# A two-block transformer kernel whose weight ring goes from four to six half slots, with the low parts written over the loaded weights

## The chip, the core and the metric

The kernel runs on one core of a Trainium2 chip. The metric is the device time of one execution in microseconds (us). The engines named below are PE (matrix multiplies; PEld is its weight load), DVE (vector), ACT (scalar, activation functions), POOL (general purpose) and SP (here it only issues the loads of the weights). Each has its own stream of instructions, run strictly in the order of the program; they wait for each other by semaphores.

## The reference

Two kinds of transformer layer, two layers of each, on 256 tokens of width 1024, everything in float32. Cut to what matters here:

```python
# first block, per layer (DEPTH = 2)
h = rms_norm(x, pre_mix_g);   x = x + rms_norm(parallel_mixer(h, ...) , post_mix_g)      # w_in, w_out
h = rms_norm(x, pre_cross_g); x = x + rms_norm(memory_cross_attention(h, mem_n, ...), post_cross_g)  # w_cq, w_ck, w_cv, w_co
h = rms_norm(x, pre_ffn_g);   x = x + rms_norm(swiglu(h, w_gate, w_up, w_down), post_ffn_g)
# second block, per layer (DEPTH = 2)
h = rms_norm_2(x, ffn1_norm); x = x + 0.5 * swiglu_2(h, ffn1_w_gate, ffn1_w_up, ffn1_w_down)
h = rms_norm_2(x, mix_norm);  (queries, keys, values, gates) = split(h @ w_in)
x = x + (g0 * (y_nsa @ w_up_nsa) + g1 * (y_sb @ w_up_sb) + g2 * (y_swa @ w_up_swa)) @ w_out
h = rms_norm_2(x, ffn2_norm); x = x + 0.5 * swiglu_2(h, ffn2_w_gate, ffn2_w_up, ffn2_w_down)
```

Nearly all of the arithmetic is products of the 256 tokens with weight matrices of width or depth 1024 or 2816.

## The kernel before, in words

All large weights are laid out by the host as one stream of 332 **slots** of 1024 x 256 numbers (1 MB), in the order in which they are needed (`ORDER`; names such as `fq0`, `wo3` are columns of a projection, `gate`, `up`, `down` with a number are parts of an FFN). Each slot is two **halves** of 512 KB, so there are 664 halves.

A float32 product is made of three faster ones: a number is split into a high part (rounded by a copy to the type fp32r) and a low part (what is left). A half therefore goes through four stations:

1. SP loads it into `raw[m % RING]` (L1874). The ring has RING = 4 such buffers.
2. ACT copies it to `w_hi` (`split_hi`, L779).
3. DVE writes `raw - w_hi` to `w_lo` (`split_lo`, L1234).
4. PE multiplies (L259): 24 matmuls a half, and the last one counts up the semaphore `half_used`.

`w_hi` and `w_lo` are rings of four, too. In before, SP loads half m into its `raw` buffer as soon as DVE has made the low part of half m - 4 (`lo_done`), whether PE has used that half or not. ACT, ahead of splitting half m, waits for the load and for `half_used` of half m - 4, since `w_hi` is overwritten.

When a slot is split is set by hand: the program of ACT and of DVE calls `ahead(name)` where slot `name` is being used, and that splits the slot after it. In a run of projections the order on DVE is `ahead(X)`, read the result of X, `ahead(Y)`, read the result of Y. In an FFN, `ahead` stands between the activations, and the eleven `ahead(("down", j))` stand together, after the last activation. Behind the last of them follows at once what ends the layer's part: in the first block `norm_add` (ACT squares the four pairs of output tiles, DVE and PE sum them, ACT takes the root, DVE scales and adds to `x`), in the second block `half_update` (DVE scales and adds straight away), and then `norm_in` (ACT makes the high parts `xn_hi` of the next input, DVE the low parts `xn_lo`), for which PE waits. Output projections (`wo`, `co`) are four slots in a row, with their four `ahead` calls together and then `norm_add` or an addition. PE's last `down` slot is ordered so that its output pairs end one after the other (`down_made`), so that these steps can begin while PE still multiplies.

Of the kernel before, what the change touches and what calls it, by code (L numbers as in the profile page):

```python
# [7 lines left out]
F32 = mybir.dt.float32  # L8
F32R = mybir.dt.float32r
# [5 lines left out]
P = 128  # L15
# [12 lines left out]
COLS = 256  # L28
SLOT = KT * COLS
HK = KT // 2  # L30
RING = 4
N_CMP = (S - 32) // 16 + 1
N_CMP0 = (P - 32) // 16 + 1
VEC = 3 * P
# [13 lines left out]
ORDER = []  # L48
# [4 lines left out]
SLOT_AT = {name: n for n, name in enumerate(ORDER)}  # L53
N_SLOTS = len(ORDER)
# [38 lines left out]
def build(nc, A):  # L93
    T, AC, V, G, SY = nc.tensor, nc.scalar, nc.vector, nc.gpsimd, nc.sync
# [3 lines left out]
    def sb(name, shape, dt=F32):  # L98
        return nc.alloc_sbuf_tensor(name, shape, dt)[tuple(slice(None) for _ in shape)]

    def sb_at(name, shape, dt, offset):
        return nc.alloc_sbuf_tensor_at(name, shape, dt, offset=offset)[tuple(slice(None) for _ in shape)]

    base = (nc.sbuf_base + 31) // 32 * 32
    shared = 13 * 2048 + 24 * 1024 + 16384
    nc.alloc_sbuf_tensor("shared", [P, shared // 4 + 16], F32)

    proj = sb_at("proj", [P, 13, 2, COLS], F32, base)
    gates = sb_at("gates", [P, 24, S], F32, base + 13 * 2048)
# [6 lines left out]
    mem_lo = sb_at("mem_lo", [P, KT, S], F32R, base + 13 * 2048 + 24 * 1024 + 8192)  # L116
    table = sb_at("table", [P, 12, S], F32, base + 13 * 2048 + 24 * 1024)

    raw = [sb(f"raw{r}", [P, HK, COLS]) for r in range(RING)]
    w_hi = [sb(f"w_hi{r}", [P, HK, COLS], F32R) for r in range(RING)]  # L120
    w_lo = [sb(f"w_lo{r}", [P, HK, COLS], F32R) for r in range(RING)]
    x = sb("x", [P, KT, S])
    xn = sb("xn", [P, KT, S])
    xn_hi, xn_lo = sb("xn_hi", [P, KT, S], F32R), sb("xn_lo", [P, KT, S], F32R)
# [70 lines left out]
    hi_done, lo_done, half_used = sig("hi_done"), sig("lo_done"), sig("half_used")  # L195
# [575 lines left out]
    def scalar_program():  # L771
        own = sig("act_own")

        def split_hi(name):
            for m in (2 * SLOT_AT[name], 2 * SLOT_AT[name] + 1):
                AC.wait_ge(*loaded[m % RING].at(m // RING + 1))
                if m >= RING:
                    AC.wait_ge(*half_used.at(m - RING + 1))
                AC.activation(w_hi[m % RING], raw[m % RING], ACT.Copy).then_inc(*hi_done.next())  # L779

        def ahead(name):

            if SLOT_AT[name] + 1 < N_SLOTS:
                split_hi(ORDER[SLOT_AT[name] + 1])

        def load_sqrt():
            AC.activation(scale_col[:, 2:3], eps, ACT.Sqrt)
# [75 lines left out]
            AC.activation(out, probT[1][:, 1, S:2 * S], ACT.Sin).then_inc(*trig_made.next())  # L863
        AC.wait_ge(*vec_made.at(1))
        AC.activation(vec_sb, bank[1][0:12, 0:VEC], ACT.Copy, scale=8.0).then_inc(*vec_copied.next())
        split_hi(ORDER[0])

        for L in range(DEPTH):
            at = lambda name: ("b1", L, name)
# [142 lines left out]
        for L in range(DEPTH, 2 * DEPTH):  # L1012
# [51 lines left out]
            m = mix_out.at(7 * l + 4)  # L1064
# [157 lines left out]
    def vector_program():  # L1222
# [8 lines left out]
        def split_lo(name):  # L1231
            for m in (2 * SLOT_AT[name], 2 * SLOT_AT[name] + 1):
                V.wait_ge(*hi_done.at(m + 1))
                V.tensor_tensor(w_lo[m % RING], raw[m % RING], w_hi[m % RING].bitcast(F32), ALU.subtract  # L1234
                                ).then_inc(*lo_done.next())

        def ahead(name):
            if SLOT_AT[name] + 1 < N_SLOTS:
                split_lo(ORDER[SLOT_AT[name] + 1])

        def low_half(lo, src, hi, ready, to):

# [110 lines left out]
        for b in range(4):  # L1353
            for k in (2 * b, 2 * b + 1):
                m = V.scalar_tensor_tensor(xn[:, k, :], xn[:, k, :], c("mem_g")[:, k:k + 1], rinv[:, 0, :],
                                           ALU.mult, ALU.mult)
# [1 line left out]
            V.wait_ge(*mem_normed.last())  # L1358
            low_half(mem_lo[:, pair_of(b), :], xn[:, pair_of(b), :], mem_hi[:, pair_of(b), :], mem_hi_done.at(b + 1),
                     mem_split)  # L1360
        split_lo(ORDER[0])

        update = None
        for L in range(DEPTH):
# [49 lines left out]
            for ct in range(2):  # L1414
                w = lambda n: small[:, SM1["conv_w"].start + 2 * n + ct:SM1["conv_w"].start + 2 * n + ct + 1]
                m = V.tensor_scalar(xc[:, ct, :], lx[:, ct, :], w(3), small_1("conv_b")[:, ct:ct + 1], ALU.mult, ALU.add)
# [453 lines left out]
    def sync_program():  # L1870
        for m in range(2 * N_SLOTS):
            if m >= RING:
                SY.wait_ge(*lo_done.at(m - RING + 1))
            SY.dma_start(raw[m % RING], A["stream"][m].rearrange("p (k c) -> p k c", k=HK)  # L1874
                         ).then_inc(*loaded[m % RING].next())

# [174 lines left out]
```

## Time and profile before

| | |
|---|---|
| median of 3 runs | 2480.09 us (2479.8 to 2481.58) |
| the profiled execution | 2480.8 us; span of the profile 2478.9 us |
| mean granted TensorE clock | 0.948 |
| PE busy | 2221.4 us (90%) |
| DVE busy | 1430.3 us (58%) |
| ACT busy | 1137.6 us (46%) |
| POOL busy | 83.8 us (3%) |
| loads of the stream | 664 of 512 KB, 144 GB/s read over the span |

Busy time is the time in which the engine had an instruction running. Only PE is near the whole span; the other engines are on the path where PE waits for them. Times in rows of a timeline are us from the span's start.

### The profile page before, as it was taken

What the parts mean: (1) busy time and instruction counts of PE and PEld (TensorE: products, weight loads), DVE (VectorE), ACT (ScalarE), POOL (GpSimd) and SP (SyncE); (2) the same over time, 40 slices, a digit from 0 to 9 for tenths busy, and PEclk for the clock granted to TensorE, in tenths of its full rate; (3) what the DMA queues carried; (4) which work ended last, traced back from release to release, by engine and by line L of the source; (5) the groups of instructions that cost most, each with busy time, mean ns of one, the idle gap of its engine ahead of it and who ended that gap; (6) DMA issues with size and microseconds to landing.
All of it is one profiled execution on the core that took longest, in us unless ns stands there. A gap on an engine that the chain in (4) does not pass through costs nothing.

```text
span 2478.9 us, 40437 instructions
## 1 busy us (share of the span) xinstructions
PE 2221.4 (90%) x17158; PEld 2126.7 (86%) x17158; DVE 1430.3 (58%) x2194; ACT 1137.6 (46%) x1745; POOL 83.8 (3%) x81
## 2 busy tenths in 40 slices
PE   3888879998988799979998998899999988988999
PEld 2877779998868799979997877899899988878999
DVE  3454656546546565465557556655556575556654
ACT  3354444443545444444445456444444444465442
POOL 4000000000000000010000000000000000000000
PEclk9888899998989999989999899999999998989999
DMA  5632425554423255645644223456456543234554
GB/s 131 188 102 84 137 83 179 186 187 136 131 74 130 96 164 181 204 145 184 200 141 153 86 79 109 158 184 194 150 187 193 165 153 102 86 103 133 176 186 153
DMA packets 97956, 360.28 MB, mean 145 GB/s; under 512 B 11064, under 2 KB 11065, under 8 KB 97264
## 3 DMA queue, kind: packets, MB, share of 16 engines
q1 hardware_dynamic: 95616, 348.17, 43.4%
q0 software_dynamic: 1728, 6.38, 1.3%
q8 instruction: 135, 2.21, 0.4%
q10 hardware_dynamic: 432, 3.15, 0.3%
q14 instruction: 45, 0.37, 0.0%
HBM read 354.25 MB, written 3.41 MB: 144 GB/s over the span
## 4 chain that ended last, share of the span: by engine, by line
PE 74%; DVE 13%; ACT 7%; issue 2%; POOL 2%; DMA 2%; ACTq 0%; DVEq 0%; POOLq 0%
PE bank L259 65%; DVE w_lo L1234 3%; ACT w_hi L779 2%; PE bank L311 1%; POOL sq L1803 1%; DMA raw<-in_stream 1%; PE bank L295 1%; PE bank L639 1%; DVE sq L1287 1%; DVE xn_lo L1260 1%; PE bank L316 1%; DVE x L1291 1%; DVE sq L1771 1%; PE bank L312 1%; ACT sq L790 0%
## 5 line engine op out<-in xcount | busy, mean ns | idle before, releaser
L259 PE MATMUL bank<-xn_hi,w_hi 128*128 128x256 f32 x3296 | 959.1, 291 | 136.6 <-DVE xn_lo L1260 103.9
L1234 DVE TENSOR_TENSOR w_lo<-raw,w_hi 128x1024 fp32r<-128x1024 f32 x664 | 809.9, 1252 | 470.1 <-ACT w_hi L779 469.9
L259 PE MATMUL bank<-xn_lo,w_hi 128*128 128x256 f32 x3296 | 950.2, 288 | 0.0
L259 PE MATMUL bank<-xn_hi,w_lo 128*128 128x256 f32 x3296 | 949.1, 288 | 0.0
L779 ACT ACTIVATE w_hi<-raw 128x1024 fp32r<-128x1024 f32 x664 | 674.2, 1050 | 339.2 <-PE bank L259 321.0
L259 PEld LDWEIGHTS bank<-xn_hi,w_hi 128*128 128x128 f32 x3296 | 651.4, 198 | 151.7 <-issue 137.7
L259 PEld LDWEIGHTS bank<-xn_lo,w_hi 128*128 128x128 f32 x3296 | 651.4, 198 | 0.2
L259 PEld LDWEIGHTS bank<-xn_hi,w_lo 128*128 128x128 f32 x3296 | 650.6, 197 | 0.0
L259 PE MATMUL bank<-hid_hi,w_hi 128*128 128x256 f32 x1056 | 291.5, 276 | 0.0
L259 PE MATMUL bank<-hid_lo,w_hi 128*128 128x256 f32 x1056 | 291.5, 276 | 0.0
L259 PE MATMUL bank<-hid_hi,w_lo 128*128 128x256 f32 x1056 | 291.5, 276 | 0.0
L259 PEld LDWEIGHTS bank<-hid_lo,w_hi 128*128 128x128 f32 x1056 | 198.3, 188 | 0.0
L259 PEld LDWEIGHTS bank<-hid_hi,w_hi 128*128 128x128 f32 x1056 | 198.3, 188 | 0.0
L259 PEld LDWEIGHTS bank<-hid_hi,w_lo 128*128 128x128 f32 x1056 | 198.2, 188 | 0.0
L831 ACT ACTIVATE hid_hi<-act_t 128x512 fp32r<-128x512 f32 x66 | 41.7, 632 | 206.0 <-DVE act_t L1305 206.0
L827 ACT ACTIVATE act_t<-act_t 128x512 f32<-128x512 f32 x66 | 41.7, 632 | 197.8 <-DVE act_t L1300 197.8
L259 PE MATMUL bank<-y_hi,w_hi 128*128 128x256 f32 x384 | 110.3, 287 | 12.2 <-DVE y_lo L1244 4.5
L259 PE MATMUL bank<-y_lo,w_hi 128*128 128x256 f32 x384 | 109.2, 284 | 0.0
L1803 POOL TENSOR_TENSOR sq<-sq 128x512 f32<-128x512 f32 x36 | 55.9, 1553 | 1574.7 <-ACT sq L790 1571.2
L259 PE MATMUL bank<-y_hi,w_lo 128*128 128x256 f32 x384 | 109.1, 284 | 0.0
L259 PEld LDWEIGHTS bank<-y_hi,w_hi 128*128 128x128 f32 x384 | 74.2, 193 | 14.6 <-issue 7.1
L1305 DVE TENSOR_TENSOR act_t<-act_t,bank 128x512 f32<-128x512 f32 x66 | 45.3, 686 | 63.7 <-PE bank L259 63.7
(338 smaller groups left out, 2562.8 us busy)
## 6 DMA issues: line engine op xcount, KB each, us to landing
raw<-in_stream SPq DMA_DIRECT2D x664, 512.0 KB, 4.2
skew<-logit POOLq DMA_DIRECT2D x1, 2304.0 KB, 35.2
table<-skew POOLq DMA_DIRECT2D x1, 1408.0 KB, 7.4
logit<-in_small POOLq DMA_DIRECT2D x4, 288.5 KB, 3.1
con<-in_con ACTq DMA_DIRECT2D x1, 1029.0 KB, 7.1
xn<-in_mem ACTq DMA_DIRECT2D x1, 1024.0 KB, 11.6
x<-in_x ACTq DMA_DIRECT2D x1, 1024.0 KB, 14.9
out<-x POOLq DMA_DIRECT2D x1, 1024.0 KB, 4.2
```

Source lines behind the costliest of these rows:

```text
L259: m = T.matmul(out, a, b, start=first and j == 0, stop=True, skip_group_check=True)
L295: m = T.matmul(out, avg, sq[:, k, :], start=k == 0, stop=k == 1)
L311: T.matmul(out, v_of(0), pT[:, 0:S], start=first, stop=False, skip_group_check=True)
L312: return T.matmul(out[:, P:S], v_of(1), pT[:, S:S + P], start=False, stop=last, skip_group_check=True)
L316: m = T.transpose(dst[:, to * P:(to + 1) * P], src[:, frm:frm + P], c("ident"))
L639: T.matmul(out[:, LATE], q[:, P:S], k, start=True, stop=True)
L779: AC.activation(w_hi[m % RING], raw[m % RING], ACT.Copy).then_inc(*hi_done.next())
L827: AC.activation(act_t, act_t, ACT.Silu).then_inc(*silu_made.next())
L831: AC.activation(hid_hi[:, 2 * j:2 * j + 2, :], act_t, ACT.Copy).then_inc(*hid_hi_made.next())
L1234: V.tensor_tensor(w_lo[m % RING], raw[m % RING], w_hi[m % RING].bitcast(F32), ALU.subtract).then_inc(*lo_done.next())
L1305: V.tensor_tensor(act_t, act_t, dense[1], ALU.mult).then_inc(*up_read.next())
L1803: G.tensor_tensor(sq[:, 0:2, :], sq[:, 0:2, :], sq[:, pair_of(b), :], ALU.add).then_inc(*summed.next())
```

## The change

RING becomes 6. `w_lo[r]` gets the same addresses as `raw[r]`: DVE subtracts in place, so the low part overwrites the loaded half, and one buffer stands for two. Since the buffer now holds what PE reads, SP may load half m only when PE has used half m - 6 (`half_used`), where it waited for `lo_done` of half m - 4. ACT's own wait for `half_used` is dropped: the load that it waits for implies it. `ahead(name)` now splits the slot two after `name`, and both ORDER[0] and ORDER[1] are split ahead of the first layer.

```diff
-RING = 4
+RING = 6
...
-    nc.alloc_sbuf_tensor("shared", [P, shared // 4 + 16], F32)
+    nc.alloc_sbuf_tensor("shared", [P, shared // 4 + 16 + RING * SLOT // 2], F32)
...
-    raw = [sb(f"raw{r}", [P, HK, COLS]) for r in range(RING)]
+    raw_at = base + shared + 64
+    raw = [sb_at(f"raw{r}", [P, HK, COLS], F32, raw_at + r * SLOT * 2) for r in range(RING)]
     w_hi = [sb(f"w_hi{r}", [P, HK, COLS], F32R) for r in range(RING)]
-    w_lo = [sb(f"w_lo{r}", [P, HK, COLS], F32R) for r in range(RING)]
+
+    w_lo = [sb_at(f"w_lo{r}", [P, HK, COLS], F32R, raw_at + r * SLOT * 2) for r in range(RING)]
...
                 AC.wait_ge(*loaded[m % RING].at(m // RING + 1))
-                if m >= RING:
-                    AC.wait_ge(*half_used.at(m - RING + 1))
                 AC.activation(w_hi[m % RING], raw[m % RING], ACT.Copy).then_inc(*hi_done.next())
...
-            if SLOT_AT[name] + 1 < N_SLOTS:
-                split_hi(ORDER[SLOT_AT[name] + 1])
+            if SLOT_AT[name] + 2 < N_SLOTS:
+                split_hi(ORDER[SLOT_AT[name] + 2])
...
-        split_hi(ORDER[0])
+        for n in range(2):
+            split_hi(ORDER[n])
...
             if m >= RING:
-                SY.wait_ge(*lo_done.at(m - RING + 1))
+                SY.wait_ge(*half_used.at(m - RING + 1))
```

(The same two edits are made for `split_lo` on DVE.) What moves on the engines is seen at three places. In these rows `raw2_66` and `w_lo2_72` are `raw[2]` and `w_lo[2]`; lines are those of the kernel in question.

SP, the loads behind the first ones, before:

```order
L1874 DMA raw3<-in_stream 128x1024
L1874 DMA raw0<-in_stream 128x1024 [waits lo_done]
L1874 DMA raw1<-in_stream 128x1024 [waits lo_done]
L1874 DMA raw2<-in_stream 128x1024 [waits lo_done]
L1874 DMA raw3<-in_stream 128x1024 [waits lo_done]
```

and now:

```order
L1876 DMA raw3_67<-in_stream 128x1024
L1876 DMA raw4_68<-in_stream 128x1024
L1876 DMA raw5_69<-in_stream 128x1024
L1876 DMA raw0_64<-in_stream 128x1024 [waits half_used]
L1876 DMA raw1_65<-in_stream 128x1024 [waits half_used]
```

Two more loads go out without a wait, and all later ones wait for PE in place of DVE.

ACT, the end of the second block's first FFN (the last two `ahead` calls of the `down` slots, then `norm_in`), before:

```order
L779 ACTIVATE w_hi0<-raw0 128x1024 [waits half_used,loaded0]
L779 ACTIVATE w_hi1<-raw1 128x1024 [waits half_used,loaded1]
L779 ACTIVATE w_hi2<-raw2 128x1024 [waits half_used,loaded2]
L779 ACTIVATE w_hi3<-raw3 128x1024 [waits half_used,loaded3]
L787 ACT_TABLE_LOAD
L787 ACTIVATE scale_col<-eps_t 128x1
L799 ACTIVATE xn_hi<-x,small 128x256 [waits x_updated]
```

and now:

```order
L779 ACTIVATE w_hi0<-raw0_64 128x1024 [waits loaded0]
L779 ACTIVATE w_hi1<-raw1_65 128x1024 [waits loaded1]
L779 ACTIVATE w_hi2<-raw2_66 128x1024 [waits loaded2]
L779 ACTIVATE w_hi3<-raw3_67 128x1024 [waits loaded3]
L787 ACT_TABLE_LOAD
L787 ACTIVATE scale_col<-eps_t 128x1
L799 ACTIVATE xn_hi<-x,small 128x256 [waits x_updated]
```

The number of splits in front of `norm_in` is the same; they are of the slots one further on, and each waits for a load alone. That load itself waits for PE.

DVE, the first projections (`proj` from bank0 and bank1 are the results of `fq0` and `fq1`), before:

```order
L1234 TENSOR_TENSOR w_lo2<-raw2,w_hi2 128x1024 [waits hi_done]
L1234 TENSOR_TENSOR w_lo3<-raw3,w_hi3 128x1024 [waits hi_done]
L1266 RECIPROCAL scale<-root 128x256 [waits rooted]
L1268 RECIPROCAL scale_col<-scale_col 128x2
L1234 TENSOR_TENSOR w_lo0<-raw0,w_hi0 128x1024 [waits hi_done,dve_own]
L1234 TENSOR_TENSOR w_lo1<-raw1,w_hi1 128x1024 [waits hi_done]
L1378 TENSOR_TENSOR proj_49<-bank0,scale 128x512 [waits half_used]
L1378 TENSOR_TENSOR proj_49<-bank1,scale 128x512 [waits half_used]
```

and now:

```order
L1235 TENSOR_TENSOR w_lo4_74<-raw4_68,w_hi4 128x1024 [waits hi_done]
L1235 TENSOR_TENSOR w_lo5_75<-raw5_69,w_hi5 128x1024 [waits hi_done]
L1267 RECIPROCAL scale<-root 128x256 [waits rooted]
L1269 RECIPROCAL scale_col<-scale_col 128x2
L1235 TENSOR_TENSOR w_lo0_70<-raw0_64,w_hi0 128x1024 [waits hi_done,dve_own]
L1235 TENSOR_TENSOR w_lo1_71<-raw1_65,w_hi1 128x1024 [waits hi_done]
L1380 TENSOR_TENSOR proj_49<-bank0,scale 128x512 [waits half_used]
L1380 TENSOR_TENSOR proj_49<-bank1,scale 128x512 [waits half_used]
```

The pair of splits in front of the first `proj` was halves 4 and 5 and is now halves 6 and 7, whose loads can only start when PE has used halves 0 and 1.

## Rows read from the trace of the kernel before

**Rows 1.** Waits, whole program: us in total, times, longest

```profile
ACT w_hi L779 <- PE bank L259: 321.0, 193, 3.7
...
PE bank L259 <- DVE xn_lo L1260: 103.9, 12, 26.2
...
PE bank L259 <- DVE w_lo L1234: 32.5, 28, 3.2
...
ACT w_hi L779 <- DMA raw<-in_stream: 18.1, 5, 6.8
```

**Rows 2.** Stretches of gate/up and down slots: us, busy per engine, PEclk, DMA, GB/s

```profile
370.00:490.00 120.00, 119.70 (x995) 119.43 (x994) 72.06 (x74) 54.87 (x65) 0.00 (x0) 1.00 0.57 184
490.00:552.00 62.00, 62.00 (x548) 61.96 (x546) 30.99 (x29) 26.72 (x28) 0.00 (x0) 1.00 0.64 204
```

**Rows 3.** Tile raw, loads' landing in stretches 500:545, 331:350, 42:58

```profile
DMA to landing us min/median/max: 4.2/4.3/4.8
...
DMA to landing us min/median/max: 3.2/3.3/3.7
...
DMA to landing us min/median/max: 22.0/23.1/27.8
```

**Rows 4.** Timelines of ACT, DVE, PE at 1256 to 1266: start, us, what, [idle before]

```profile
1256.91 1.06 ACT L779 ACTIVATE w_hi<-raw 128x1024 fp32r<-128x1024 f32 x1 [1.66 <-PE bank L259]
...
1258.01 1.23 DVE L1234 TENSOR_TENSOR w_lo<-raw,w_hi 128x1024 fp32r<-128x1024 f32 x1 [1.49 <-ACT w_hi L779]
1259.15 0.68 DVE L1329 SCALAR_TENSOR_TENSOR sq<-bank,scale 128x512 f32<-128x512 f32 x1
...
1264.94 0.36 PE L259 MATMUL bank<-xn_hi,w_hi 128*128 128x256 f32 x1 [2.69 <-DVE xn_lo L1260]
```

**Rows 5.** Timeline of ACT, 546 to 553

```profile
546.81 1.06 ACT L779 ACTIVATE w_hi<-raw 128x1024 fp32r<-128x1024 f32 x1 [1.66 <-PE bank L259]
547.89 1.28 ACT L787 ACT_TABLE_LOAD   x1
...
552.19 0.60 ACT L790 ACTIVATE sq<-bank 128x512 f32<-128x512 f32 x1 [0.76 <-PE bank L259]
```

**Rows 6.** Timeline of ACT, 262 to 268

```profile
262.12 1.06 ACT L779 ACTIVATE w_hi<-raw 128x1024 fp32r<-128x1024 f32 x1 [1.82 <-PE bank L259]
...
264.61 1.56 ACT L790 ACTIVATE sq<-bank 128x512 f32<-128x512 f32 x3
267.82 0.60 ACT L790 ACTIVATE sq<-bank 128x512 f32<-128x512 f32 x1 [1.66 <-PE bank L259]
```

**Rows 7.** Timelines of ACT and DVE, 120 to 127

```profile
120.13 1.06 ACT L779 ACTIVATE w_hi<-raw 128x1024 fp32r<-128x1024 f32 x1 [0.38 <-PE bank L259]
...
122.37 0.41 DVE L1391 TENSOR_TENSOR act_t<-bank,scale 8x256 f32<-8x256 f32 x1
...
126.56 0.49 ACT L886 ACTIVATE act_t<-act_t,small 8x256 f32<-8x256 f32 x1
```

**Rows 8.** Timeline of PE and POOL, the first 75 us; DMA issues

```profile
46.77 0.55 PE L259 MATMUL bank<-xn_hi,w_hi 128*128 128x256 f32 x1 [26.17 <-DVE xn_lo L1260]
...
74.28 0.58 PE L259 MATMUL bank<-xn_hi,w_hi 128*128 128x256 f32 x1 [11.64 <-DVE proj L1378]
...
40.38 1.21 POOL L1844 DMA_DIRECT2D skew<-logit  x1 [1.12 <-ACT logit L865]
...
skew<-logit POOLq DMA_DIRECT2D x1, 2304.0 KB, 35.2
```

**Rows 9.** Waits of PE, 1296:1356, and busy time of 1310:1325

```profile
PE bank L259 <- DVE w_lo L1234: 6.1, 5, 3.2
PE bank L612 <- ACT root L1029: 2.6, 1, 2.6
...
1310.00:1325.00 15.00, 11.44 (x78) 10.43 (x79) 13.73 (x21) 4.96 (x6) 0.00 (x0) 0.89 0.47 147
```

**Rows 10.** Timeline of PE, 1967 to 1976

```profile
1970.59 0.55 PE L259 MATMUL bank<-xn_hi,w_hi 128*128 128x256 f32 x1 [2.69 <-DVE xn_lo L1260]
```

More of the change, by code:

```diff
@@ L1237, in ahead @@
         def ahead(name):
-            if SLOT_AT[name] + 1 < N_SLOTS:
-                split_lo(ORDER[SLOT_AT[name] + 1])
+            if SLOT_AT[name] + 2 < N_SLOTS:
+                split_lo(ORDER[SLOT_AT[name] + 2])
         def low_half(lo, src, hi, ready, to):
@@ L1360, in vector_program @@
                      mem_split)
-        split_lo(ORDER[0])
+        for n in range(2):
+            split_lo(ORDER[n])
         update = None
```

## The prediction

> **What bounds the kernel now.** I read the list of waits first. PE is busy for 90% of the span, so the question is what it waits for. Its longest wait is for `xn_lo`, the input of the next group of projections: 103.9 us in 12 places. Waits for a low part of a weight, which an earlier split could remove, are 32.5 us in 28 places [rows 1]. The same list says how the weights are fed: ACT waits 193 times, 321.0 us together, for PE to free a half, but only 5 times, 18.1 us, for a load. In before, loads are so far ahead that nobody sees them.
>
> Next the stretches. In gate/up slots PE runs 995 matmuls in 120 us with no gap, in down slots 548 in 62 us [rows 2]. With 24 matmuls a half, that is 2.89 and 2.72 us a half, 5.8 and 5.4 us a slot, and the granted clock is 1.00. There is nothing to win inside these runs. Time is lost at their ends, where the timelines show ACT or DVE still splitting weights and turning to the next step as soon as they are done: the last split ends on DVE at 1259.2, and the update of x begins in the same moment [rows 4].
>
> **The step that decides.** In after, `ahead(name)` splits slot n+2, whose second half takes the buffer of slot n-1's second half. In before, the same call splits slot n+1 into the buffer of that same half. So ACT and DVE reach the same point of their programs, and wait for PE to finish the same half. But before, the data lay ready; now its load is issued only then. Each split that was released by PE is released one transfer later. The transfer takes 4.3 us in a stretch of down slots and 3.3 us in one of output slots [rows 3].
>
> **Inside a dense run this is hidden.** From `half_used` to the low part: 3.3 or 4.3 for the load, 1.06 on ACT, 1.23 on DVE, some 0.1 between them, so 5.7 to 6.7 us, while PE needs the half five halves later, 13.6 to 14.4 us. Reads of results that stand behind the split come at most 1 us late, and PE has a slot of slack for them. The cover would be gone with a transfer of over 11 us.
>
> **At the end of a run it isn't.** What follows the last `ahead` there is late by the transfer, less what ACT or DVE waited for anyway:
>
> - Second block, end of an FFN with another stage behind it, three times (the last FFN has no slot left to split). ACT's last copy starts at 1256.91, the moment PE frees the half. In after it starts 4.35 later, and so does DVE's 1259.15 update; DVE is at work without a break from there to the `xn_lo` that lets PE start at 1264.94 [rows 4]. +4.35 each, **+13.1**.
> - First block, end of the FFN, twice. ACT's copy at 546.81 is followed by a table load of 1.28 and four squares, the last of which begins at 552.19, when PE is done [rows 5]. In after: 546.8 + 4.35 + 1.06 + 1.28 + 0.1 = 553.6, and three squares at 0.52 (three take 1.56 [rows 6]) put the last at 555.2. +3.0 each, **+6.0**.
> - First block, `wo` and `co`, four times. Same reckoning from 262.12 with transfers of 3.3 to 3.8: the last square at 262.1 + 3.3 + 1.06 + 1.28 + 0.1 + 1.56 = 269.4 to 269.9, for 267.82 [rows 6]. +1.9 each, **+7.6**.
> - Second block, `wo`, twice. ACT waits there for the whole slot in any case. Copy and table load end 3.3 + 1.06 + 1.28 = 5.6 after the half, the slot after 5.8. What is left is one addition of x on DVE, about 0.6. **+1.2**, bounds 0 and 2.6 (the latter if the load takes 4.3 and a second addition is late).
> - The forget gate `f`, twice. Its read on DVE, at 122.37, stands behind a split released by PE at 120.1; with a load of about 4.6 (three loads are asked for 1.4 us apart) it comes at 127.1, and PE's `fv1` and ACT's 126.56 step wait for it [rows 7]. ACT had slack of 4 us; 0.6 to 1.2 remains. **+1.8**.
>
> **The start.** Two more halves are split on DVE ahead of the first norm, 2 x 1.23, so the first matmul moves from 46.77 to 49.2. That is only delay ahead of a stall: PE waits until 74.28 for `proj`, which waits for halves 4 and 5, loaded in 22 to 28 us while the `skew` write runs, 35.2 us from 40.4 [rows 3, 8]. In after those two come early, but the split ahead of that `proj` is of halves 6 and 7, asked for when PE has used halves 0 and 1, near 55 and 58, and the write runs to 75.6. Best case, a load with nothing before it lands by 70; worst, at 81. I take 74.1, which with 1.06, 1.23 and two reads gives 76.7. **+2.4**, bounds -1 and +6.
>
> **What the earlier split gains.** Of the 32.5 us of [rows 1], 6.1 lie in the second block's run from `sk` to `sv`, and as much in the second layer. But DVE is busy 13.7 of 15 us there and PE's next wait, for ACT's root, already takes 2.6 [rows 9]: most of what PE wins it waits for one step later. The exception is the copy of `nv`, for which ACT waits; it comes earlier. Followed through, the root comes 2.5 to 3 us sooner. I take 2.5 a layer, **-5.0**, bounds -7 and -1. The other waits for low parts stand in front of a wait for the same DVE (`merged`, the first softmax) and give nothing.
>
> **Clock.** Longer gaps mean more restarts at the lower level. The same gap of 2.69 is followed once by a matmul of 0.36 and once by one of 0.55 [rows 4, 10]. A half at 1.2 GHz takes some 5 us for 2.9. At two or three places a gap of 3 grows to 5 to 7. **+2**, bounds 0 and 6.
>
> In-place writing I cost at nothing: the subtraction reads and writes as many bytes as before, in 1.23 us, and PE's slots cover it; if it took 0.1 us more or less, only the 13 places above would show it, 1 us in all. The dropped ACT wait is replaced by the longer one.
>
> **Sum.** 13.1 + 6.0 + 7.6 + 1.2 + 1.8 + 2.4 - 5.0 + 2.0 = 29.1 on the profiled execution's 2480.8, which is 0.7 above the median. 2509.9, or **2509 us** against the median, 1.2% slower.
>
> **A rule.** The Trainium skill (DMA: Bandwidth & Descriptors, Rules for kernel authors) says to issue a DMA early and wait for it late, so that its fixed cost overlaps with compute. This change issues later and leaves the wait where it was; the trace agrees in so far as only 5 waits for loads are seen in before. Another page (SBUF, State Buffer, The DMA setup-cost knee) fits 2 us plus bytes over 436 GB/s, an estimate of 3.2 us for 512 KB wherever it is issued. By that figure the sum would be some 6 us less.
>
> **Rivals.**
>
> 1. The transfer is 3.3 us at the FFN ends, too. The 3.3 was seen between runs of output slots; that the down slots show 4.3 may come from the loads of before being released by DVE. Five ends give back 1.05 each, and the four `wo`/`co` ends 0.2: 2503. Chance 0.18; I would call it half right.
> 2. **Faster.** PE's 28 waits for low parts all vanish (-32.5) and pass nothing on to the root or `merged`, and halves 6 and 7 land by 70 (-1). Against the 29.7 us of the ends and 2 of the clock that is still no gain, so the loads must also be hidden in part: it is decided where the transfer adds under 2.2 us at the five FFN ends, which halves their 19.1. Then 2470. DVE's 13.7 of 15 us [rows 9] speak against it, the 28 waits for it. Chance 0.07.
> 3. **No change.** The first half of that alone: 2480.8 + 31.7 - 33.5 = 2479. Chance 0.06.
> 4. Load-paced runs. If loads spaced 2.72 us apart queue up once they start with PE, each by more than the one before, PE waits within down slots. 100 halves at +0.5 us give 2560. The 204 GB/s of [rows 2] are sustained at the same spacing, so this needs the spacing to break. Chance 0.03.
>
> The forecast itself has 0.66. The others that are slower bring that side to 0.87. A change of 0.2%, 5 us, is about what can be told from none. Bounds of the terms, not all taken at once: low, 2509 less 6 (loads, rival 1), 2 (gain), 3 (start) and 2 (clock), so 2496; high, plus 4 (start), 4 (clock), 4 (gain), 3 (ends), so 2524. I take 2495 to 2524, which leaves out rivals 2 to 4, 0.16.
>
> **What the profile would show.** ACT's waits for `raw` go from 18 us to over 500, those for PE's halves vanish from L779. PE's wait for `xn_lo` rises from 104 to about 130 in about as many places; its wait for `w_lo` falls below 5, and that for L612's root grows to 5 or more. The loads' landing stays at 3 to 4.4 us. At the end of the second block's first FFN the gap of 2.69 is about 7. I am wrong if these gaps don't grow, or if PE waits within gate/up/down runs.

## The result and the profile after

The changed kernel takes 2521.64 us, median of 4 runs (2513.07 to 2522.56), against 2479.95 us for the kernel before on the same chip (4 runs, 2479.68 to 2481.58). The ratio is 1.0159, with a 95% interval of 1.0136 to 1.0182: slower by 1.6%, where 1.2% was predicted. The profiled executions have spans of 2520.5 and 2478.9 us, so 41.6 us are to be found. The mean granted clock fell from 0.948 to 0.933.

The list of waits of the changed kernel (us in total, times, longest us):

```profile
engine line waited for: us in total, times, longest us
...
ACT w_hi L779 <- DMA raw<-in_stream: 536.0, 334, 16.0
...
PE bank L261 <- DVE xn_lo L1261: 118.7, 12, 28.4
...
PE bank L297 <- DVE sq L1252: 39.3, 7, 16.3
...
PE bank L614 <- ACT root L1030: 9.4, 2, 4.8
...
PE bank L261 <- DVE w_lo L1235: 5.2, 2, 2.6
```

ACT's 193 waits for PE [rows 1] are gone, and 334 waits for a load stand in their place. PE gained on low parts (32.5 us in 28 places before, 5.2 in 2 now) and lost on `xn_lo` (118.7 for 103.9), on `sq` before the mean-square matmuls (39.3 for 25.7), and on the root (9.4 for 5.2).

Inside the dense runs nothing is lost, as the windows show (the columns are those of [rows 2]; the first is a run of gate and up slots, the second one of down slots):

```profile
core 0: us, PE busy (x) PEld busy (x) DVE busy (x) ACT busy (x) POOL busy (x), PEclk, DMA share, GB/s
380.00:500.00 120.00, 120.00 (x1003) 120.00 (x1002) 73.35 (x74) 56.68 (x65) 0.00 (x0) 1.00 0.54 182
500.00:552.00 52.00, 52.00 (x460) 52.00 (x460) 24.86 (x22) 20.70 (x20) 0.00 (x0) 1.00 0.59 195
```

PE works through 120 and 52 us without a gap at full clock. The time went at the ends. This is the end of the first FFN of the second block, ACT's, DVE's and PE's timelines, 25.7 us later than in [rows 4]:

```profile
1282.57 1.06 ACT L779 ACTIVATE w_hi<-raw 128x1024 fp32r<-128x1024 f32 x1 [0.63 <-DMA raw<-in_stream]
...
1283.66 1.22 DVE L1235 TENSOR_TENSOR w_lo<-raw,w_hi 128x1024 fp32r<-128x1024 f32 x1 [0.46 <-ACT w_hi L779]
1284.81 0.68 DVE L1330 SCALAR_TENSOR_TENSOR sq<-bank,scale 128x512 f32<-128x512 f32 x1
...
1290.60 0.55 PE L261 MATMUL bank<-xn_hi,w_hi 128*128 128x256 f32 x1 [5.91 <-DVE xn_lo L1261]
```

ACT's last copy now waits for a load; everything behind it stands in the same order and takes as long as before, and PE's gap of 2.69 us has become 5.91.

The end of a first-block FFN and one `wo` end, for which the row of the kernel before is the one in the third fence:

```profile
558.66 1.06 ACT L779 ACTIVATE w_hi<-raw 128x1024 fp32r<-128x1024 f32 x1 [2.01 <-DMA raw<-in_stream]
559.74 1.28 ACT L787 ACT_TABLE_LOAD   x1
...
561.14 2.04 ACT L790 ACTIVATE sq<-bank 128x512 f32<-128x512 f32 x4
...
564.58 2.08 PE L297 MATMUL bank<-sq,avg 128*128 128x256 f32 x4 [4.12 <-DVE sq L1252]
```

```profile
274.10 2.07 PE L297 MATMUL bank<-sq,avg 128*128 128x256 f32 x4 [3.49 <-DVE sq L1252]
```

```profile
269.20 1.13 PE L295 MATMUL bank<-sq,avg 128*128 128x256 f32 x4 [1.42 <-DVE sq L1251]
```

At the `wo` end PE's gap grew from 1.42 to 3.49, the 1.9 us that had been worked out and a little more; at the FFN end it grew from 1.41 to 4.12. But the four short matmuls behind the gap of 3.49 then took 2.07 us for 1.13. The granted clock of these matmuls was 0.50, where it had been 1.00 (the first window is of the changed kernel, the second of the one before):

```profile
274.10:276.17 2.07, 2.07 (x4) 1.17 (x4) 0.00 (x0) 0.00 (x0) 0.00 (x0) 0.50 0.00 0
```

```profile
269.20:270.33 1.13, 1.13 (x4) 0.67 (x4) 0.00 (x0) 0.00 (x0) 0.00 (x0) 1.00 0.00 0
```

The gap is paid twice: once as idle time and once as lower clock.

Two stretches of the second block's projections. The first fence is the changed kernel, three rows of PE and then two of ACT, from the projection `wkv` to the gate matmuls; the second is the same last step of the kernel before:

```profile
1346.27 0.36 PE L261 MATMUL bank<-xn_hi,w_hi 128*128 128x256 f32 x1 [2.59 <-DVE w_lo L1235]
...
1362.01 0.60 PE L575 MATMUL bank<-logit,small 128*64 128x15 f32 x8 [4.22 <-ACT logit L1042]
...
1378.95 6.81 PE L614 MATMUL bank<-small,x 128*128 128x24 f32 x32 [4.82 <-ACT root L1030]
...
1374.28 1.06 ACT L779 ACTIVATE w_hi<-raw 128x1024 fp32r<-128x1024 f32 x1 [1.65 <-DMA raw<-in_stream]
1375.36 1.28 ACT L1038 ACT_TABLE_LOAD   x1
```

```profile
1354.35 5.38 PE L612 MATMUL bank<-small,x 128*128 128x24 f32 x32 [2.63 <-ACT root L1029]
```

PE gains 4.85 us on the kernel before at `wq`, and then waits for DVE's split of `wkv` (2.59), for ACT's `logit` (4.22, a wait that the kernel before does not have) and for the root (4.82 for 2.63), after which 32 small matmuls take 6.81 us for 5.38. The table load in front of the root stands behind a copy that waited for a load.

To add up I took, for each of the 664 half slots, the end of PE's last matmul on it in both traces, and followed how the difference steps:

| place | predicted us | measured us |
|---|---|---|
| start, to the end of `fk0`'s first half | +2.4 | +3.3 |
| `wo` and `co` ends, first block, 4 | +7.6 | +12.5 (3.03, 3.12, 3.09, 3.29) |
| FFN ends, first block, 2 | +6.0 | +8.6 (4.04, 4.52) |
| FFN ends into and in the second block, 3 | +13.1 | +13.7 (4.65, 3.97, 5.12) |
| `nq0` to `nq1`, 2 | none | -5.2 (-4.5, -0.75) |
| `nq1` to `sv`, 2 (the gain) | -5.0 | +9.9 (+3.6, +6.2) |
| `f`, second-block `wo`, clock, rest | +5.0 | -1.2 |
| sum | 29.1 | 41.6 |

The measured column is the difference of two single profiled executions, and steps of a few us at single places don't all come from the program. The kernel with `ahead(v1)` moved (below) has the program of the changed one throughout the first block, yet it is 4.6 us later at the second layer's `fv1`. The kernel with DVE's work cut has the same program as the changed one in `bg10` and `bg11`, and differs there by +4.8 and -4.0 us. The second half of `wkv` takes either 4.11 or 7.68 us. So a step is read as an effect below where it comes back at all places of a kind, or is far over these.

### The profile page after: what moved, and what is told of

It is laid out like the page before. It is cut to its first block, busy times and chain, and to the rows that moved or that the text cites. A ratio compares the mean times of both kernels' runs of the same rounds, so it can differ in the third digit from the quotient of the medians.

```text
span 2520.5 us, 39777 instructions
## 1 busy us (share of the span) xinstructions
PE 2236.4 (89%) x17158; PEld 2140.3 (85%) x17158; DVE 1440.5 (57%) x2194; ACT 1153.2 (46%) x1745; POOL 84.5 (3%) x81
## 4 chain that ended last, share of the span: by engine, by line
PE 71%; DVE 14%; ACT 8%; DMA 4%; issue 2%; POOL 1%; DVEq 0%; ACTq 0%; POOLq 0%
PE bank L261 63%; DMA raw<-in_stream 3%; DVE w_lo L1235 3%; ACT w_hi L779 2%; PE bank L313 1%; PE bank L297 1%; PE bank L641 1%; DVE xn_lo L1261 1%; POOL sq L1805 1%; DVE sq L1288 1%; PE bank L318 1%; DVE rinv L1576 1%; DVE sq L1773 1%; DVE sq L1252 1%; PE bank L314 1%
## 5 line engine op out<-in xcount | busy, mean ns | idle before, releaser
L1235 DVE TENSOR_TENSOR w_lo<-raw,w_hi 128x1024 fp32r<-128x1024 f32 x664 | 824.0, 1255 | 687.4 <-ACT w_hi L779 687.1
L261 PE MATMUL bank<-xn_hi,w_hi 128*128 128x256 f32 x3296 | 961.0, 292 | 150.4 <-DVE xn_lo L1261 118.7
L779 ACT ACTIVATE w_hi<-raw 128x1024 fp32r<-128x1024 f32 x664 | 689.8, 1053 | 536.4 <-DMA raw<-in_stream 536.0
L1245 DVE TENSOR_TENSOR hid_lo<-act_t,hid_hi 128x512 fp32r<-128x512 f32 x66 | 45.7, 692 | 51.0 <-ACT hid_hi L831 51.0
## 6 DMA issues: line engine op xcount, KB each, us to landing
x<-in_x ACTq DMA_DIRECT2D x1, 1024.0 KB, 14.9
```

Source lines behind the costliest of these rows:

```text
L261: m = T.matmul(out, a, b, start=first and j == 0, stop=True, skip_group_check=True)
L1245: V.tensor_tensor(lo, src, hi.bitcast(F32), ALU.subtract).then_inc(*to.next())
```

## Experiments

All ratios are to the kernel before, timed beside the experiment on the same chip. Its median was 2480.5 beside the first four experiments (through both runs held), 2479.7 beside the next four that ran there, and 2486.0 (18 runs, 2475.0 to 2488.3) on a second chip, that of the two kernels with DVE's work cut, of seven and five, and of eight and four with `ahead(v1)` moved. So kernels are compared by ratio.

**One slot ahead, ring of six in place.** Both `ahead` functions split the next slot again:

```diff
-            if SLOT_AT[name] + 2 < N_SLOTS:
-                split_hi(ORDER[SLOT_AT[name] + 2])
+            if SLOT_AT[name] + 1 < N_SLOTS:
+                split_hi(ORDER[SLOT_AT[name] + 1])
...
-        for n in range(2):
+        for n in range(1):
```

> The six half slots and the in-place low parts stay; ahead(name) splits one slot ahead again and only ORDER[0] is split ahead of the first norm. The load of a half is then issued two halves (5.4 to 5.8 us) before the point at which ACT comes to it. Theory (the exposed transfer at the ends of the runs): the 41 us go away altogether; the start even gains, since halves 4 and 5 are loaded before the skew write: 2470 to 2482 us. Rival A (the buffer that is held until PE is done, or the write in place, costs by itself): stays near 2520. Rival B (half each): near 2500.

2473.78 us, ratio 0.9973 (0.9961 to 0.9985), in the range expected. All 41.6 us are gone, and a little more. At the start PE's wait before `fk0` is lost and one before `fk1` takes its place, of 8.35 us:

```profile
75.34 0.55 PE L261 MATMUL bank<-xn_hi,w_hi 128*128 128x256 f32 x1 [8.35 <-DVE w_lo L1235]
```

The six buffers in place do no harm; with six buffers, the loss needs the second slot of lead.

**A load released half a slot later still.** In `sync_program`:

```diff
-                SY.wait_ge(*half_used.at(m - RING + 1))
+                SY.wait_ge(*half_used.at(m - RING + 2))
```

> The changed kernel with each load issued one half later: SP waits until PE has used half m - 5 (for m - 6). Theory: each end of a run is later by one more half, 2.7 us at the five FFN ends and 2.9 at four wo/co ends, two wo ends of the second block, two ends of cq, two f, two ahead of the gate products of the second block: some 13.6 + 11.5 + 6 x 2.9 to 8 x 2.9 = 42 to 48 us, so 2562 to 2572. PE's runs themselves stay without gaps. If the ends are late for another reason than the load: 2520 to 2530.

2674.27 us, ratio 1.0777 (1.0761 to 1.0793), far over what was expected: the direction was right, the size was not. ACT's and PE's waits:

```profile
ACT w_hi L779 <- DMA raw<-in_stream: 820.4, 416, 17.1
...
PE bank L297 <- DVE sq L1252: 62.1, 7, 17.1
```

At the five FFN ends the steps are another 4.1 to 6.5 us each, at the four `wo` and `co` ends of the first block 2.0 to 4.1. The surprise is in the first block's memory projections, where steps of 1.8 to 8.9 us appear that no theory had named. By the program, the load of a slot's second half now waits for the slot that ACT and DVE are about to serve, so loads, splits and reads would follow one another in a ring; this reading was not tested. PE also waits inside a run of gate and up slots, against what was expected: 103.79 us busy of the 120 from 380 to 500, for 120.00 in the changed kernel. The run shows how steep the cost is when the release moves one half, not how large the original one was.

**The last split of a down run held back.** The last `ahead` of a run of down slots is called behind `norm_in`, and the one after it behind `norm_scale`, on both engines:

```diff
+            if held:
+                held.append(name)
+                name = held.pop(0)
             if SLOT_AT[name] + 2 < N_SLOTS:
                 split_hi(ORDER[SLOT_AT[name] + 2])
...
+        def run_of(names, hold):
+
+            for name in names[:-1]:
+                ahead(name)
+            if hold and SLOT_AT[names[-1]] + 2 < N_SLOTS:
+                held.append(names[-1])
+            else:
+                ahead(names[-1])
...
-            for j in range(FB):
-                ahead((f, "down", j))
+            run_of([(f, "down", j) for j in range(FB)], True)
```

> The changed kernel, still two slots ahead, but the last ahead of the eleven down slots is made behind norm_in, and the one after it behind norm_scale. Theory: the five FFN ends give back what the slots' end times show there, 4.0 + 4.5 + 4.65 + 4.0 + 5.1 = 22 us: 2499. wo and co ends stay as late as they were (3.1 each). If the lateness is not from these splits: 2520.

2509.68 us, ratio 1.0113 (1.0096 to 1.013). The five ends gave back 3.6, 4.6, 5.5, 5.8 and 7.5 us, 27 in all for the 22.3 that they had cost, so these terms do come from the splits in front of `norm_in`. More came back than was lost because the hold also takes the split's own time out of the way (PE's gap before `nq0` is 1.79 us, where the kernel before has 2.69), and because PE's first half of `nq0` in the second layer took 3.12 us for 5.47 (2.35 of the 7.5); how much is the load alone, this run doesn't separate. Only 14 us arrive at the end of the span: two splits now stand in front of the first reads of the next stage (`fk0` +3.7, `nq1` +1.1 and +3.7), and steps at `cv0` to `cv2`, places where kernels of the same program differ by as much, add 3. The expectation, 2499, had left that out.

**`wo` and `co` runs held too**, the same with `run_of(..., True)` on these.

> As e3, and the last ahead of each wo and co run is held back as well. Theory: four times 3.1 us more and some 1 us at the second block's wo: 2486. What is left over before (6 us) is the start (3.3) and the second block's projections (10 by the slots' end times, part of it clock), less what comes back there by chance.

2496.08 us, ratio 1.006 (1.0045 to 1.0075), 10 us over the 2486 expected. That is the 11 us missed in the run before: from there to here it is 13.6 us, where 13.4 had been expected. The four ends give back 3.4, 3.5, 3.2 and 3.5, and the row of the `wo` end is again that of the kernel before:

```profile
272.43 1.13 PE L297 MATMUL bank<-sq,avg 128*128 128x256 f32 x4 [1.41 <-DVE sq L1287]
```

**Only `wo` and `co` held.**

> The changed kernel with only the last ahead of the wo and co runs held back (until behind norm_in; the one after it until behind norm_scale), the down runs as in the changed kernel. Theory: each end is a stall of its own, and the four ends of wo and co in the first block and two of wo in the second give back 3.1 to 3.5 and about 1 us each, as they did when both kinds were held: 13.6 us less than the changed kernel, 2508 us, range 2505 to 2511. Rival: the gain of holding both came from their being held together (a later wait absorbs one alone): 2515 us or more.

2512.84 us, ratio 1.0129 (1.0115 to 1.0143), a little above the range. The four ends give back 3.11, 3.19, 3.12 and 3.32, 12.7 us; the second block's two `wo` ends give nothing where 2 had been expected, and later steps cost the rest. Held alone these four ends are worth about the same as together, so each is a stall of its own.

**Ring of four in place, one slot ahead.**

```diff
-RING = 6
+RING = 4
...
-                split_hi(ORDER[SLOT_AT[name] + 2])
+                split_hi(ORDER[SLOT_AT[name] + 1])
...
-        for n in range(2):
+        for n in range(1):
```

(The last two edits are made on DVE, too.)

> This is the changed kernel with the ring at four half slots and the splits one slot ahead (the ring of the kernel before, but with the low part written over the weights, so that the load of half m waits until PE has read half m-4). Theory: the stalls come from the relation between ring and lead, not from six buffers or from two slots of lead: in a call of ahead(n) the split waits for a load that the end of slot n-1 released, exactly as in the changed kernel. So the eleven named ends (FFN, wo, co) end as late as there: about 12.5 + 8.5 + 13.7 us at those, and with one slot less of cover at least as much elsewhere: 2510 to 2535 us. Rival: it is the second slot of lead, or where in SBUF the six buffers lie; then this kernel has neither and runs as before, near 2480 us, plus at most the start.

2526.38 us, ratio 1.0191 (1.0168 to 1.0214). This kernel has neither six buffers nor the second slot of lead, only the low parts written over the weights, and it is as slow as the changed one: the two intervals overlap. At the four `wo` and `co` ends its steps are 3.0 to 3.3 us, as there; at the FFN ends, with the half slots just before them, 3.1 to 4.7 for 4.0 to 5.1. Its list of waits has 338 waits of ACT for loads (334 there), and its `wo` end the same row:

```profile
ACT w_hi L779 <- DMA raw<-in_stream: 542.5, 338, 16.7
```

```profile
277.68 2.08 PE L297 MATMUL bank<-sq,avg 128*128 128x256 f32 x4 [3.50 <-DVE sq L1252]
```

So the loss comes with the relation alone, once it is PE that releases a buffer: ring less lead leaves no slot in which a load can run before its split is called.

**Rings of different lengths.** The same 12 buffers, but eight for weights and low parts and four for high parts; one slot ahead; ACT waits for PE's half m-4 again:

```diff
-RING = 6
+RING = 8
+HI_RING = 4
...
-                AC.activation(w_hi[m % RING], raw[m % RING], ACT.Copy).then_inc(*hi_done.next())
+                if m >= HI_RING:
+                    AC.wait_ge(*half_used.at(m - HI_RING + 1))
+                AC.activation(w_hi[m % HI_RING], raw[m % RING], ACT.Copy).then_inc(*hi_done.next())
```

> Weights and low parts share a ring of eight half slots, the high parts have one of four (12 buffers, as before and after), splits one slot ahead, ACT waits again until PE has read half m-4, loads wait for half m-8. Theory: a load is released two slots before its split is called, so no split waits for a landing outside the start, and the ends are as in the kernel before. At the start halves 6 and 7 are loaded ahead of the write of the skew table as 4 and 5 were in the run with one slot ahead and six; PE gets one slot (5.4 us) further before it waits for a load that runs beside that write. 2473.8 - 5.4 = 2468 us, range 2464 to 2472. Rival: the loads that now run beside the skew write delay it and all that waits for it, or the wait moves on to the next slot whole: 2474 us or more.

2468.64 us, ratio 0.9953 (0.994 to 0.9965), within 1 us of what was expected. It is faster than the kernel before, and no version tried is clearly faster than it. Its waits:

```profile
ACT w_hi L782 <- PE bank L262: 315.6, 191, 3.7
...
ACT w_hi L782 <- DMA raw<-in_stream: 12.8, 5, 10.9
```

These are nearly the figures of [rows 1] again. Set against the kernel before, half by half, this one is 11.6 us ahead at `rq` and 11.7 us ahead at the end of the program: the gain is all made at the start, and the 2388 us behind it run as before. Writing in place costs nothing here. The wait that is left at the start is

```profile
76.51 0.36 PE L262 MATMUL bank<-xn_hi,w_hi 128*128 128x256 f32 x1 [3.00 <-DVE w_lo L1238]
```

**Seven and five** instead of eight and four.

> As the kernel with eight low and four high, but a ring of seven half slots for weights and low parts and one of five for the high parts: ACT never waits for PE's reading, loads are released half a slot later, and one half slot less is loaded ahead of the skew write at the start. Theory: a load is still released a slot and a half before its split, so nothing is exposed but the start: half 7 comes beside the skew write, which costs the same as halves 6 and 7 did in the run with one slot ahead and six (PE needs both), 2472 to 2474 us. Rival: what counts is that ACT is free of PE: then below 2466 us.

2474.85 us on a chip whose kernel before took 2486.03, ratio 0.9956 (0.9935 to 0.9977). By the ratio it can't be told from eight and four, where 2472 to 2474, 3 to 5 us more, had been expected. Its trace has the step that was expected, `fk1` 8.0 later and `rq` 3.05 earlier than there, 5.2 us in sum with what lay before. One premise did not hold: ACT was not freed from PE, its waits only fell from 191 to 168:

```profile
ACT w_hi L782 <- PE bank L262: 275.6, 168, 2.7
```

What a free ACT would be worth is therefore not shown.

**The changed kernel with `ahead(v1)` behind `head_norm(4)`.**

```diff
-            ahead(at("v1"))
             cmp_hidden_of(1)
             head_norm(4, 1)
+            ahead(at("v1"))
```

(That is ACT's program; DVE's has the same move.)

> The changed kernel with one ahead moved in the second block: ahead(v1), which splits bg0, stands behind head_norm(4) in ACT's and DVE's programs and no longer in front of the table load and root in it. Theory: that split waits for a load that the end of nv releases, so root, DVE's chain behind it and PE's norm matmuls (gap 4.8 us for 2.6, then 32 small matmuls in 6.8 us for 5.4) are late by it; 2.1 to 3.6 us a layer come back: 2514 to 2518 us. Rival: PE's gap there is set by another chain (DVE's own work), or the split of bg0 is then late for PE: no change, 2521 us, or up to 2525.

2515.76 us, in the range expected, ratio 1.0149 (1.0127 to 1.0172), whose interval overlaps that of the changed kernel: the total doesn't show it. The place does. From the end of `nv` to that of `sv` the kernel before takes 19.34 and 19.28 us in its two layers, the changed one 22.71 and 23.02, this one 19.62 and 19.65. The row of the gate matmuls:

```profile
1381.70 5.92 PE L614 MATMUL bank<-small,x 128*128 128x24 f32 x32 [1.78 <-ACT root L1030]
```

Of the 6.5 us, other steps (the clock in `wkv` among them, below) took most back in the profiled execution, which ends 1.3 us ahead of the changed kernel's. Kernels with the same code in this place differ by up to 1.5 us there, so 3.1 and 3.4 are clear, but not to a tenth.

**DVE's work cut**, in the changed kernel and in the one before: the reciprocal of `head_norm(1)` takes 4 columns.

```diff
-                V.reciprocal(rinv_f[:, 0:w * S], root_f[:, 0:w * S]).then_inc(*own.next())
+                full = 4 if n == 1 else w * S
+                V.reciprocal(rinv_f[:, 0:full], root_f[:, 0:full]).then_inc(*own.next())
```

> The changed kernel with one piece of DVE's work left out: the reciprocal in head_norm(1) of the second block takes 4 columns for 512 (3.35 us less, twice in the program; the other columns of rinv are those of an earlier call). Theory: in the second block's projections of the changed kernel DVE's chain is the bound; PE's lead of 4.85 us at wq ends in a wait of 4.2 us at cmp_out_of(0), because the copies that it waits for stand behind DVE's reading of wkv, and the changed kernel therefore cannot keep what its earlier splits give. With 3.3 us less of DVE in front of the reading of wq and wkv, the end of nv comes 3.3 us earlier in each layer: 6 to 7 us off the changed kernel, 2515 us, range 2512 to 2518. Rival: PE or the loads are what sets the end of nv: nothing gained, 2521 us.

> The kernel before with the same piece of DVE's work left out (4 columns for 512 in the reciprocal of head_norm(1)). Theory: there DVE's next step (reading wq) waits for PE already (0.20 us), so the 3.35 us only lengthen that wait: within 1 us of the kernel before, 2479 to 2481 us. Rival: DVE bounds that stretch in the kernel before as well; then 6 us less, 2474 us.

The changed kernel so cut takes 2515.93 us, ratio 1.0124 (1.0101 to 1.0147), against 1.0159 uncut; the two intervals overlap a little. The kernel before so cut takes 2483.39 us, ratio 0.9994 (0.9979 to 1.0008): nothing. By place it is clearer. From the end of `nq1` to that of `nv`, first and second layer:

| kernel | us | us |
|---|---|---|
| before | 63.94 | 63.66 |
| before, DVE cut | 63.95 | 63.94 |
| changed | 64.19 | 66.17 |
| changed, DVE cut | 62.14 | 62.28 |

In the kernel before, DVE only waits longer for PE, 3.36 us for 0.20; this is its row in the cut one:

```profile
1322.08 0.69 DVE L1569 TENSOR_TENSOR proj<-bank,scale 128x512 f32<-128x512 f32 x1 [3.36 <-PE bank L259]
```

In the changed kernel the cut saves 2.05 and 3.9 us there. The 3.9 is not all DVE's: the second half of `wkv` takes 4.11 us for 7.68 in that layer, and in the changed kernel and three of its variants the stretch takes 64.2 us where that half takes 4.11 and 66.1 to 66.2 where it takes 7.68. That leaves some 2 us a layer for the cut, of the 3.35 taken out. PE's wait for the split of `wkv` is gone, though the wait for `logit` stays, 3.89:

```profile
1362.32 0.62 PE L575 MATMUL bank<-logit,small 128*64 128x15 f32 x8 [3.89 <-ACT logit L1042]
```

So before, PE paced this stretch, and in the changed kernel DVE's chain does, for about 2 us of it.

**Eight and four with `ahead(v1)` behind `head_norm(4)`.**

> Eight low and four high, one slot ahead, and ahead(v1) (which here splits sv) behind head_norm(4). Theory: in front of the root of head_norm(4) stand 2.0 us of ACT's splits; PE's gap before its 32 gate matmuls is 2.6 us and ends with the root; moved, the root comes 2.0 us earlier and sv's low parts are there by the end of those matmuls (5.4 us): 2 us a layer, 2464.6 us, range 2462 to 2467. Rival: the next wait (scores and their tables behind sv) takes it back: 2468 us.

2473.07 us, ratio 0.995 (0.9932 to 0.9969); without the move 0.9953. A miss. PE's gap before the gate matmuls fell only from 2.61 to 1.78. The waits behind `sv` are those of the kernel without the move. The matmuls behind the gap then decide. These are the two layers of this kernel, and the second layer of the one without the move:

```profile
1341.52 4.65 PE L615 MATMUL bank<-small,x 128*128 128x24 f32 x32 [1.78 <-ACT root L1033]
...
2043.67 6.85 PE L615 MATMUL bank<-small,x 128*128 128x24 f32 x32 [1.78 <-ACT root L1033]
```

```profile
2044.97 4.59 PE L615 MATMUL bank<-small,x 128*128 128x24 f32 x32 [2.61 <-ACT root L1033]
```

From the end of `nv` to that of `sv` the first layer gains 0.9 us (18.43 for 19.36), and the second loses 0.85 (20.13 for 19.28).

## Why the prediction was right, and where it was not

The time of 2521.64 us lies within the range of 2495 to 2524, near its upper end. Part of that is luck. By the table, the terms that were too low miss 23.9 us (14.9 of it the gain, 4.9 the `wo` and `co` ends), and 11.4 us that nobody had counted on came the other way: 5.2 between `nq0` and `nq1`, 6.2 in the last line. Without these the time would have been about 2533.

**The mechanism** was right: each split that PE released is released one transfer later, dense runs hide it, ends of runs don't. The ring of four shows that the relation between ring and lead, with PE as the one that releases, makes the loss without six buffers or a longer lead, and the ring of eight and four that the loss goes when the relation is restored and everything else stays.

**FFN ends into and in the second block**, 13.1 predicted, 13.7 measured. At two of the three the last load took 4.25 and 4.30 us, as expected. The gaps grew by 3.2, 4.2 and 4.2 us, 11.7 for the 13.1; the clock of PE's first half behind them made the other 2.1 (+1.4, -0.2, +0.9), so the near agreement is partly chance. At the first end the load took only 3.27, and ACT's last copy and PE's start moved by as much (they are 25.7 us later than before, where the down slots ahead of them are 22.4 us later); another 1.4 us came with the clock, since PE's first half there ran at a granted clock of 0.63 behind the longer gap, where it had run at 1.00. These windows are the first 4.4 us of the changed kernel's `nq0` and the first 3.1 of that of before:

```profile
1290.60:1295.00 4.40, 4.40 (x25) 4.40 (x26) 2.81 (x6) 3.19 (x8) 1.17 (x1) 0.63 0.00 0
```

```profile
1264.90:1268.00 3.10, 3.06 (x24) 2.92 (x24) 2.86 (x6) 1.89 (x5) 0.00 (x0) 1.00 0.00 0
```

The prediction had not seen what follows either: from `nq0` to `nq1` 4.5 and 0.75 us come back. In the first layer PE's gap before the mean matmuls shrank from 1.95 to 0.84 us, and the first half of `nq1`, which had run at the lower level, runs at the full one. The two windows, of before and of the changed kernel, are

```profile
1276.00:1281.00 5.00, 5.00 (x25) 5.00 (x25) 4.39 (x5) 2.43 (x4) 0.00 (x0) 0.50 0.19 72
```

```profile
1301.00:1304.00 3.00, 3.00 (x27) 3.00 (x27) 2.46 (x4) 2.37 (x4) 0.00 (x0) 1.00 0.00 0
```

**`wo`, `co` and first-block FFN ends**, 13.6 predicted, 21.1 measured. The terms were mis-sized. The growth of the gap was near (2.0 to 2.1 for 1.9 at `wo` and `co`, 2.7 and 3.5 for 3.0 at the FFN ends; 14.5 in all), but each end also pays 0.94 us more in the four matmuls behind the gap, 5.7 us over six ends. That belonged in these terms and not in a general 2 us for the clock. What is left, 0.0 to 0.4 us an end, was not followed up.

**The gain**, -5.0 predicted, +9.9 measured, is the step that failed: "Followed through, the root comes 2.5 to 3 us sooner." Its premise, that ACT's copy of `nv` comes earlier, fell: PE doesn't reach the end of `nv` earlier (64.2 us from the end of `nq1` for 63.9 in the first layer, 66.2 for 63.7 in the second), since DVE's chain paces the stretch, as the cut reciprocal showed, and PE's lead is spent at `wkv` and `cmp_out_of(0)`. Some 2 of the 2.5 us lost in the second layer go with the slow half of `wkv`. And the prediction had not priced the last `ahead` in front of the root, which meets the same transfer as the ends of runs: moving it gave back 3.1 and 3.4 us locally, of the 3.4 and 3.7 lost there. DVE's 13.73 busy us of 15 [rows 9] had been read, and had been used only for the other waits.

**The start**, +3.3 for +2.4: the wait for `proj` went on, as predicted; half 7 landed at 75.1, where 74.1 had been taken. The wait for the forget gate appeared (`fv1` +1.8 and +2.8) but the next step, `rv`, gave 1.9 and 2.0 back; the second block's `wo` ends show no step of their own.

**Rivals.** Rival 1 is borne out in part: at the five FFN ends the last load took 3.58, 4.37, 3.27, 4.25 and 4.30 us, so near 3.3 at two of five, and 3.22 to 3.34 at the four `wo` and `co` ends. The 4.3 us does not belong to down slots, nor to a release by DVE: the median load of a down run's halves took 3.25 and 3.31 us in two of the changed kernel's six runs and 4.28 to 4.32 in the other four, 3.38 in one of six of the kernel before, and 3.3 in five of six of the ring of eight and four. What decides between the two is open. At the ends where the load was short, the clock took more than this gave back. Rivals 2 and 3 needed the 28 waits for low parts to go and pass nothing on. They went, 32.5 to 5.2 us, and were passed on. Rival 4 did not come: PE has no gap in the runs shown. Of the signs named, the waits for loads (536, over 500) and the end of those for PE's halves came, and the gap grew, to 5.91 in the first layer and 6.93 in the second for about 7; `xn_lo` was 118.7 for about 130, `w_lo` 5.2 for below 5, the root's 4.8 for 5.

**What stays open.** Why the second half of `wkv` runs at half clock in the second layer of the changed kernel (window below, 3.6 us) and not in its first; in the kernel with `ahead(v1)` moved it does so in both layers, with DVE's work cut in neither, and with only `wo` and `co` held in the first and not in the second, though the code of that stretch is the same in all but the cut one.

```profile
2067.00:2074.50 7.50, 7.50 (x37) 7.50 (x36) 6.23 (x4) 3.08 (x4) 0.00 (x0) 0.50 0.23 73
```

## What to carry to other kernels

A ring's length is worth only what is left after the lead: count, for the call that consumes a load, which release the load waited for, and if it is the release that the call itself waits for, the whole transfer is exposed wherever the program turns from one stage to the next. When one buffer is written over another, its release moves to the later reader; if memory is fixed, give the buffer with the long life (here weights and low parts) the long ring and the other the short one. A lead that is gained on one engine was worth nothing here, since the next engine was busy for 13.7 of 15 us.

## What the hardware showed that was not expected

- Short matmuls pay for the gap before them. In the first block, four mean-square matmuls took 1.13 us behind gaps of up to 1.42 us and 2.07 or 2.08 behind gaps of 3.44 to 4.90; the 32 gate matmuls took 5.38 behind 2.63, 6.81 behind 4.82. For the gate matmuls it is not one curve: behind 1.78 they took 5.92 in one kernel and 4.65 and 6.85 in the two layers of another, and the kernel before itself took 5.38 and 4.62 behind 2.63 and 2.62.
- The clock also gives back: the same half slot of `nq1` took 5.5 us at 0.50 in the kernel before and 3.1 at 1.00 in the changed one, where the gap before the mean matmuls ahead of it was 0.84 for 1.95.
- The subtraction in place takes 1.22 to 1.23 us, as out of place.
- A load of 512 KB takes about 3.3 or about 4.3 us, by the stretch, in runs of the same kind of slots.
